# Nine and seven ring places, other stage ends, a moved low part, and the last expert behind the overflow branch, in a fused two-block kernel

## The reference, cut to what matters

```
first block:   x += pool_mixer(rms_norm(x));   x += hier_moe(rms_norm(x))        layer 0: pool, moe0
               x += mla_attention(rms_norm(x)); x += hier_moe(rms_norm(x))       layer 1: mla, moe1
               x = rms_norm(x, final_norm)
second block, for each of 2 layers (ffn00, mix0, ffn01 | ffn10, mix1, ffn11):
    x = x + 0.5 * rmsnorm(swiglu(rmsnorm(x, g0)), g1)          D_FF = 2816
    x = x + rmsnorm(mixer(rmsnorm(x, g2)), g3)                 4 attention heads, 4 mLSTM heads
    x = x + 0.5 * rmsnorm(swiglu(rmsnorm(x, g4)), g5)
hier_moe: top-1 of 4 groups, top-2 of its 8 experts; each expert (silu(h @ gate) * (h @ up)) @ down, 1024 x 512
```

## Time and profile before

| | us |
|---|---|
| time, median of 3 runs | 2138.51 |
| lowest, highest | 2137.9, 2140.11 |
| the profiled execution | 2138.28 |
| its span, first to last instruction | 2136.5 |
| PE busy | 1972.4 (92%) |
| DVE, ACT, POOL busy | 824.0, 627.5, 50.8 |

### The profile page before, as it was taken

One profiled execution on the slowest core, in us unless ns is written; L12 is line 12 of the kernel. 1 busy time (PEld: TensorE's weight loads), 2 busy tenths in 40 slices (PEclk: granted clock), 3 DMA queues, 4 the chain that ended last, 5 costly groups with the idle time before them and its releaser, 6 DMA issues.

```text
span 2136.5 us, 38361 instructions
## 1 busy us (share of the span) xinstructions
PE 1972.4 (92%) x17260; PEld 1450.9 (68%) x17260; DVE 824.0 (39%) x1263; ACT 627.5 (29%) x1016; POOL 50.8 (2%) x103
## 2 busy tenths in 40 slices
PE   6999888988989998889979999989999999999998
PEld 5544444446774444444459988879988998877996
DVE  3111111115630111111155546865545554776552
ACT  2000000004520000000054436654435444565441
POOL 0000000000000000000000000010000000010000
PEclk8999999999999999999999999999999999999999
DMA  9999999996469999999955545326545554434552
GB/s 392 414 427 428 427 428 426 428 428 245 161 237 428 426 428 428 427 427 428 426 227 201 183 162 188 119 94 221 183 172 197 190 185 170 158 103 165 185 189 79
DMA packets 56770, 599.81 MB, mean 281 GB/s; under 512 B 6544, under 2 KB 6800, under 8 KB 9488
## 3 DMA queue, kind: packets, MB, share of 16 engines
q1 hardware_dynamic: 55440, 593.79, 70.0%
q10 hardware_dynamic: 1152, 3.41, 0.6%
HBM read 596.12 MB, written 1.05 MB: 280 GB/s over the span
## 4 chain that ended last, share of the span: by engine, by line
PE 64%; DMA 21%; DVE 6%; ACT 5%; issue 3%; POOL 1%; SPq 0%; DVEq 0%; POOLq 0%; ACTq 0%
PE PS L517 14%; PE PS L519 13%; PE PS L518 13%; DMA RING<-in_w_down 11%; PE PS L660 11%; PE PS L630 6%; DMA RING<-in_w_up 4%; DMA WK<-in_w_down 3%; PE PS L605 2%; ACT SPLIT L1315 1%; DMA WK<-in_w_up 1%; ACT JK L1309 1%; PE PS L688 1%; DMA RING<-in_units 1%; DVE SPLIT L1796 1%
## 5 line engine op out<-in xcount | busy, mean ns | idle before, releaser
L1796 DVE TENSOR_TENSOR SPLIT<-RING,SPLIT 128x2048 fp32r<-128x2048 f32 (+2 forms) x178 | 400.7, 2257 | 247.1 <-ACT SPLIT L1315 246.9
L660 PE MATMUL PS<-RING,WK 128*32 128x512 f32 x816 | 373.7, 613 | 58.7 <-DMA RING<-in_w_down 38.5
L517 PE MATMUL PS<-HTH,SPLIT 128*128 128x256 f32 x1344 | 383.9, 286 | 0.0
L519 PE MATMUL PS<-HTH,SPLIT 128*128 128x256 f32 x1344 | 380.3, 283 | 0.0
L518 PE MATMUL PS<-HTL,SPLIT 128*128 128x256 f32 x1344 | 380.3, 283 | 0.0
L1315 ACT ACTIVATE SPLIT<-RING 128x2048 fp32r<-128x2048 f32 (+2 forms) x178 | 334.1, 1886 | 138.4 <-DMA RING<-in_units 129.4
L660 PEld LDWEIGHTS PS<-RING,WK 128*32 128x32 f32 x816 | 87.9, 113 | 306.8 <-issue 274.3
L517 PEld LDWEIGHTS PS<-HTH,SPLIT 128*128 128x128 f32 x1344 | 257.8, 192 | 1.9 <-issue 1.3
L518 PEld LDWEIGHTS PS<-HTL,SPLIT 128*128 128x128 f32 x1344 | 257.9, 192 | 0.5
L519 PEld LDWEIGHTS PS<-HTH,SPLIT 128*128 128x128 f32 x1344 | 257.8, 192 | 0.0
L630 PE MATMUL PS<-RING,WK 128*32 128x128 f32 x7104 | 231.0, 274 | 3.6 <-DMA RING<-in_w_up 3.2
(11 more groups left out here) (321 smaller groups left out, 2001.5 us busy)
## 6 DMA issues: line engine op xcount, KB each, us to landing
RING<-in_units SPq DMA_DIRECT2D x171, 1024.0 KB, 4.8
RING<-in_w_gate SPq DMA_DIRECT2D x56, 2048.0 KB, 25.5
RING<-in_w_up SPq DMA_DIRECT2D x55, 2048.0 KB, 26.2
RING<-in_w_down SPq DMA_DIRECT2D x53, 2048.0 KB, 29.3
WK<-in_w_down SPq DMA_DIRECT2D x9, 2048.0 KB, 31.6
WK<-in_w_up SPq DMA_DIRECT2D x9, 2048.0 KB, 26.1
WK<-in_w_gate SPq DMA_DIRECT2D x8, 2048.0 KB, 26.7
RING<-in_w_down SPq DMA_DIRECT2D x3, 1024.0 KB, 21.7
```

The source lines that it names most:

```text
L517: pe.matmul(out, ll, rh, start=start, stop=False)
L519: return pe.matmul(out, lh, rh, start=False, stop=stop)
L660: t = pe.matmul(PS[32 * i:32 * i + 32, 4 + h, :], mo.HE[:, pb, 32 * f:32 * f + 32], v[:, c, 512 * h:512 * h + 512], start=f == 0, stop=f == 3)
L1796: dv.tensor_tensor(unit_part(u, 1), loaded(u), unit_part(u, 0).bitcast(F32), ALU.subtract).then_inc(s_lo, 1)
```

## The change

It does the following.

- **The ring** has nine places in the MoE stages and seven in the others (NS = 9, HOME = 7). Two places then lie in WK, which grows from 13440 to 14112 columns. Room for it comes from the SBUF area that is set aside for dynamic DMA (`dynamic_dma_scratch_size=1024`) and from S and G, which hold two groups of four experts in turn in place of 32 experts. `places` and `gates` run for one group at steps 1, 5, 9, ...
- **The overflow branch** stands ahead of step 31 on ACT and DVE in both MoE stages, and on PE in moe0. Steps 31 and 32 (and DVE's last adds, PE's last combine) stand in both ways.
- **The entry of ffn00**: DVE's product with the final gain stands in the MoE stage, behind the adds of its own block. ACT squares X and that product before hi(u0 + 1).
- **The end of a stage**: ACT squares the PSUM row in two halves of 512, and DVE multiplies the halves with the gain row (`gains`), the two engines on different halves. The root is applied in the pass that adds to X (`add`), in two halves with semaphores of their own; ACT squares X by halves. POOL sums two partial sums. halves(1) stands ahead of hi and lo of the fifth unit; behind a mixer lo(u0 + 1) and lo(u0 + 2) are each later by one step.
- **The mixer**: lo(u0 + 14) stands behind decayed(3).
- **The last stage**: PE finishes the left half of block 1's columns first, and X leaves in four transfers.

```diff
-NS = 7
-HOME = 6
+NS = 9
+HOME = 7
+WORK = 14112
...
-        mo.S = al(2048).rearrange("p (b n) -> p b n", b=2)
-        mo.G = al(2048).rearrange("p (b n) -> p b n", b=2)
+        mo.S, mo.G = (al(512).rearrange("p (k b n) -> p k b n", k=2, b=2) for _ in range(2))
...
-                    if s == HOME and i < NS and stage == "moe1":
+                    if s >= HOME and i < NS and stage == "moe1":
...
-                sp.wait_ge(s_x, 2 * len(STAGES) - 1 + b)
-                sp.dma_start(W["out"][128 * b:128 * b + 128, :], X[:, b, :]).then_inc(s_out, 16)
+                for h in range(2):
+                    sp.wait_ge(*((s_x, 2 * len(STAGES) - 1 + b) if h else (s_xh, 2 * len(SECOND) - 1 + b)))
+                    sp.dma_start(W["out"][128 * b:128 * b + 128, 512 * h:512 * h + 512],
+                                 X[:, b, 512 * h:512 * h + 512]).then_inc(s_out, 16)
...
+            def inverse_rms_of_halves(out, halves, q, after, done):
+                po.wait_ge(*after)
+                po.tensor_scalar(out, halves[0], halves[1], q * EPS, ALU.add, ALU.add).then_inc(own.up(), 1)
+                po.wait_ge(own.sem, own.n)
+                po.tensor_tensor(out, out, MH[:, 0:1], ALU.pow).then_inc(done, 1)
...
-            for e in range(33):
-                if e == 8:
...
+            early = 31 if l == 0 else 33
+            def end():
+                for e in range(early, 33):
+                    step(e)
+                if l == 0:
+                    combine(7)
+            for e in range(early):
+                if e == 8:
+                    over = pe.value_load(FLAG[0:1, l:l + 1], min_val=0, max_val=1)
+                step(e)
+            if l:
+                combine(7)
             with pe.If(over > 0):
+                end()
                 pe_overflow(pe, l)
+            if l == 0:
+                with pe.Else():
+                    end()
...
-            for k in range(7, 11):
-                down(k, (1,), s_unit, after if k == 10 else None)
+            if after:
+                for k in range(7, 11):
+                    down(k, (1,), s_unit, after if k == 10 else None)
+            else:
+                for h in range(2):
+                    for k in range(7, 11):
+                        hi, lo = unit_pair(u0 + 22 + k)
+                        for c in range(2):
+                            f = 2 * k + c
+                            t = three(pe, PS[:, 2 + h, :], (HFH[:, f, 128:256], HFL[:, f, 128:256]),
+                                      (hi[:, c, h * 512:h * 512 + 512], lo[:, c, h * 512:h * 512 + 512]), False, f == 21)
+                        if h:
+                            t.then_inc(s_unit, 1)
+                        elif k == 10:
+                            t.then_inc(s_half, 1)
...
+                if n < 5:
+                    x_ready(n, b)
+                    square(X[:, b, :], SM[:, b:b + 1], (s_sq, 2 * n + b + 1))
+                    return
+                for h in range(2):
+                    ac.wait_ge(*((s_x, 2 * (n - 1) + b + 1) if h else (s_xh, 2 * (n - 5) + b + 1)))
+                    square(X[:, b, 512 * h:512 * h + 512], SM[:, b + 24 * h:b + 24 * h + 1],
+                           (s_sq, 10 + 4 * (n - 5) + 2 * b + h + 1), JK[:, 512 * h:512 * h + 512], 1 / 32)
...
-                j = SECOND.index(stage)
-                ac.wait_ge(*((s_unit, end_unit(stage)) if b else (s_half, j + 1)))
-                square(PS[:, 2 * b:2 * b + 2, :], SM[:, 4 + b:5 + b], (s_psq, 2 * j + b + 1),
-                       JK[:, :].rearrange("p (a n) -> p a n", a=2))
+                j, last = SECOND.index(stage), stage == SECOND[-1] and b
+                for h in range(2):
+                    if last and h == 0:
+                        ac.wait_ge(s_half, len(SECOND) + 1)
+                    elif last or h == 0:
+                        ac.wait_ge(*((s_unit, end_unit(stage)) if b else (s_half, j + 1)))
+                    else:
+                        ac.wait_ge(s_gn, 4 * j + 2 * b + 1)
+                    square(PS[:, 2 * b + h, :], SM[:, 4 + b + 22 * h:5 + b + 22 * h], (s_psq, 4 * j + 2 * b + h + 1),
+                           JK[:, 512 * h:512 * h + 512], 1 / (32 * post_place(stage)[2]))
...
                 post(before, 1)
                 hi(u0 + 3)
                 norm(n, 1)
+                halves(stage, 1)
                 hi(u0 + 4)
-                halves(stage, 1)
             def enter(stage):
...
                     ac.activation(XS[:, b, 0:512], XS[:, b, 0:512], ACT.Copy, scale=SM[:, 2 + b:3 + b]).then_inc(s_xsa, 1)
                 hi(u0)
                 squares(n, 0)
+                gained(0)
                 hi(u0 + 1)
-                gained(0)
+                scale(0)
                 squares(n, 1)
-                scale(0)
+                halves(stage, 0)
                 gained(1)
-                halves(stage, 0)
                 hi(u0 + 2)
                 scale(1)
                 hi(u0 + 3)
...
+                for e in range(31):
+                    if e == 8:
+                        ac.wait_ge(s_flag, l + 1)
+                        over = ac.value_load(FLAG[0:1, l:l + 1], min_val=0, max_val=1)
+                    step(e)
                 with ac.If(over > 0):
+                    step(31)
+                    step(32)
...
+                with ac.Else():
+                    step(31)
+                    step(32)
...
+            def gains(stage, b):
+                j, k, last = SECOND.index(stage), post_place(stage)[0], stage == SECOND[-1] and b
+                dv.wait_ge(s_row[j % 2], 16 * (j // 2 + 1))
+                if not last:
+                    dv.wait_ge(*((s_unit, end_unit(stage)) if b else (s_half, j + 1)))
+                for h in (0, 1) if last else (1, 0):
+                    if last or h == 0:
+                        dv.wait_ge(s_psq, 4 * j + 2 * b + h + 1)
+                    dv.tensor_tensor(XS[:, b, 512 * h:512 * h + 512], PS[:, 2 * b + h, :], RB[:, k, 512 * h:512 * h + 512],
+                                     ALU.mult).then_inc(s_gn, 1)
+            def add(stage, b):
                 j = SECOND.index(stage)
-                row = RB[:, post_place(stage)[0], :].rearrange("p (a n) -> p a n", a=2)
-                dv.wait_ge(s_row[j % 2], 16 * (j // 2 + 1))
+                dv.wait_ge(s_gn, 4 * j + 2 * b + 2)
                 dv.wait_ge(s_prs, 2 * j + b + 1)
-                dv.scalar_tensor_tensor(XS[:, b, :].rearrange("p (a n) -> p a n", a=2), PS[:, 2 * b:2 * b + 2, :],
-                                        SM[:, 6 + b:7 + b], row, ALU.mult, ALU.mult).then_inc(s_pt, 1)
-                dv.wait_ge(s_pt, 2 * j + b + 1)
                 dv.wait_ge(s_fin, 2)
-                dv.tensor_tensor(X[:, b, :], X[:, b, :], XS[:, b, :], ALU.add).then_inc(s_x, 1)
+                for h in range(2):
+                    x = X[:, b, 512 * h:512 * h + 512]
+                    dv.scalar_tensor_tensor(x, XS[:, b, 512 * h:512 * h + 512], SM[:, 6 + b:7 + b], x, ALU.mult,
+                                            ALU.add).then_inc(s_x if h else s_xh, 1)
             def boundary(before, stage):
                 n, u0 = STAGES.index(stage), UNIT[stage]
-                lo(u0)
-                lo(u0 + 1)
-                post(before, 0)
+                early = 2 if before[:3] == "ffn" else 1
+                for u in range(u0, u0 + early):
+                    lo(u)
+                gains(before, 0)
+                add(before, 0)
                 norm_tail(n, 0)
-                lo(u0 + 2)
+                lo(u0 + early)
                 halves(stage, 0)
-                post(before, 1)
+                gains(before, 1)
+                if early == 1:
+                    lo(u0 + 2)
+                add(before, 1)
                 lo(u0 + 3)
                 norm_tail(n, 1)
+                halves(stage, 1)
                 lo(u0 + 4)
-                halves(stage, 1)
...
-                for b in range(2):
-                    dv.wait_ge(s_x, 2 * n - 1 + b)
-                    dv.tensor_tensor(XS[:, b, :], X[:, b, :], RB[:, 2, :], ALU.mult).then_inc(s_fg, 1)
...
+            def places(l, g):
+                if g >= 2:
+                    dv.wait_ge(s_ga, 16 * l + 2 * g - 2)
+                for b in range(2):
+                    dv.tensor_tensor(mo.S[:, g % 2, b, :].rearrange("p (e s) -> p e s", e=4),
+                                     cs("iota")[:, 0:C].unsqueeze(1).to_broadcast([128, 4, C]),
+                                     mo.PO[:, b, 4 * g:4 * g + 4].unsqueeze(2).to_broadcast([128, 4, C]),
...
-                            places(l, 1)
                             longest(l)
-                            gates(l, 1)
+                        if e % 4 == 1 and e < 29:
+                            places(l, e // 4 + 1)
+                            gates(l, e // 4 + 1)
...
                 with dv.If(over > 0):
+                    step(31)
+                    step(32)
+                    add(7, 0)
```

(20 more changed lines are left out.)

89 lines of the change are left out of this document (40 added, 49 removed).

## The result

The changed kernel takes 2108.64 us (median of 4 runs, 2105.24 to 2111.07) against 2139.31 us for the kernel before, measured beside it: a ratio of 0.9856, 95% interval 0.9839 to 0.9873. (Beside the later runs the kernel before took 2139.82 to 2140.47 us.) The profiled execution took 2108.3 us with a span of 2106.4; before it was 2138.28 and 2136.5. So 30.1 us of span are gone where 35.0 were forecast, and the time lies in the range. It is 5 us above the forecast.

A forecast was written before the change was run, and what follows sets the result against it. Transfers were taken to bound the MoE stages, and PE from 1100 us on. The terms summed to 35.0 us, taking the profiled 2138.3 us to 2103.3 us, with a range of 2094 to 2114.

The forecast's parts named there:

- ring, moe1: Start of moe1: nine slabs issued ahead of the first freed place, so two fewer to move afterwards; 9.8 us gained.
- end of moe0, branch and transfers: End of moe0: 1.9 us won by the transfers, less what PE's early branch gives back; 1.2 us gained.
- entry of mla: Start of mla: ACT's branch taken ahead of step 31, so squares and PE's transposes start earlier; 1.7 us gained.
- entry of ffn00: From moe1's end to ffn00: early branch and reordered squares and product start PE's transposes sooner; 4.0 us, from 3 to 4.4.
- three starts behind ffn: Stage starts behind the three ffn stages: halves(1) moved earlier removes PE's wait of 1.13 us at each; 3.4 us gained.
- boundaries behind the mixers: Stage starts behind both mixers: waits for XS and halves(1) go, 1.2 us lost to POOL's wait; 2.5 us each, 5.0 together.
- clock behind them: Behind the second stage start, TensorE's clock returns to its upper level after shorter idle stretches; 2.0 us gained, or none.
- mixers: In the mixers, moving lo(u0+14) behind decayed(3) brings sums(2) earlier: 3.4 us in mix0, 2.5 in mix1, together 5.9.
- The lead isn't kept: Rival: something else fills the first gap of moe1, so 9.8 us are missing; 2113.1 us, chance 0.08.
- The jump at the end of the second way: Rival: this jump stalls too, 3.5 us at ffn00's entry and 1.7 at mla's; 2108.5 us, chance 0.08.
- The gaps only move: Rival: lower clock stays in the mixers and behind the stage start, POOL's wait eats the mixer boundaries; 2112.1 us, chance 0.18.
- Slower: Rival: early-branch instruction fetches queue behind weights, costing 26 us in moe0 and 26 in moe1; 2155 us, chance 0.04.

The follow-up runs named there:

- moe0_late: Changed kernel with the overflow branches of TensorE, ScalarE and VectorE back behind their last work in moe0 alone; median 2106.34 us.
- best30: Changed kernel with ScalarE's and VectorE's branches ahead of step 30 in both MoE stages, TensorE's behind its last combine in moe0; median 2104.78 us.
- ad_late: Changed kernel with ScalarE's and VectorE's branches back behind the last adds in both MoE stages, final-gain products behind the branch; median 2115.41 us.
- again: The changed kernel once more, unaltered, as yardstick and second profile; 2108.92 us.
- pe_late: Changed kernel with only TensorE's overflow branch in moe0 back behind the last combine; median 2106.25 us.
- mixlo: Changed kernel with, behind the mixers, lo(u0 + 1) between add(0) and norm_tail(0), lo(u0 + 2) ahead of halves(0), nothing between gains(1) and add(1); 2108.93 us.
- ns7: Changed kernel with the ring back at seven places in the MoE stages and six in the others (NS 7, HOME 6); median 2119.09 us.
- ns7_scratch: Changed kernel with the ring back at NS 7, HOME 6 and the dynamic DMA scratch area at its former size; median 2119.72 us.
- ns8: Changed kernel with eight ring places in the MoE stages (NS 8, HOME 7); median 2115.06 us.
- tail_back: Changed kernel with TensorE finishing block 1 of the last stage unit by unit and the stage ending like the others, output still in four transfers; 2109.32 us.

## Why the prediction held, and which steps of it didn't

The forecast was 35.0 us of gain, term by term; the table gives 30.1:

| term | forecast | table | by experiment |
|---|---|---|---|
| ring, moe1 | 9.8 | 8.9 | 10.2 to 10.5, with moe0 |
| end of moe0, branch and transfers | 1.2 | -3.35 | early branches: a loss of 1.6 (moe0_late) to 3.9 (best30) at mla's transposes |
| entry of mla | 1.7 | 1.9 | 2.5 by ad_late, 2.7 by moe0_late |
| from mla's transposes to moe1's first freed place | 0 | 2.2 | the clock for the most part; 1.4 us apart in two profiles of the same kernel |
| entry of ffn00 | 4.0 | 3.4 | 6.4 for the branch alone |
| three starts behind ffn | 3.4 | 4.0 | 6.9 for all five |
| boundaries behind the mixers | 5.0 | 4.3 | not tried as a whole |
| clock behind them | 2.0 | 1.7 | not tried |
| mixers | 5.9 | 5.0 | 4.8 to 5.1 |
| tail | 2.0 | 2.1 | 0.8 for the column order |

- **The failed step** is the 1.2 us for the end of moe0, what the transfers win there less TensorE's early branch. The last combine came 3.35 us later instead. I had charged TensorE's branch between 0 and 1.9 us, because TensorE had 2.82 us of idle time ahead of the last expert but one, and charged nothing for ScalarE's and VectorE's early branches. Four things were wrong. First, the stall is 3.67 us, more than that idle time. Second, behind it the clock was at 0.50, and the gate and up matmuls that were left took 1.5 us more. Third, the silu of expert 31 stands behind ScalarE's branch: with TensorE's branch away it came behind 4.77 us of stall, and TensorE waited 2.50 for it. Fourth, the 1.9 us of the transfers hardly arrived. In the profile after, the slabs land 1.0 to 1.2 us earlier than before between 60 and 126 us, but the up slab of expert 31 (before: 488.8 us) only 0.3 to 0.8 us earlier, in this profile and in those of again, pe_late, ad_late, moe0_late and best30. TensorE's wait for the down slab of expert 30 ends at 493.48 us in best30 and at 493.87 before:

```profile
493.48 1.93 PE L679 MATMUL PS<-RING,WK 128*32 128x256 f32 x32 [0.93 <-DMA RING<-in_w_down]
```

What took back the rest isn't shown. Besides, all ten profiles with nine places have a stall near 480 us (1.6 to 2.2 us, best30's and moe0_late's included) that the kernel before doesn't have. The range of the term should have reached to minus 3.4.
- **Luck.** The 2.2 us from mla's transposes to moe1 were in no term, and most of them went with the clock. At mla's start it was at 0.50 for 6.8 us before and not at all in the changed kernel (0.8 us), near 580 us for 10.2 us before and 3.4 after (1.1 us; TensorE's mean granted clock in the whole stretch was 0.91 before and 0.96 after). Among the profiles with nine places the stretch takes 122.8 to 125.2 us, in best30 no less than before (125.0), so nothing shows that the change brings it. Without it 27.9 us of gain would be left.
- **The entry of mla**: the working gives 1.3 us (506.9 to 505.6), I wrote 1.7, and 1.9 it is.
- **The ring** was right in mechanism and size. The 0.9 us less in the two profiles is about what two profiles of one kernel differ by (0.8).
- **The entry of ffn00**: the transposes are 4.13 us nearer, 4.0 were forecast. 0.7 us is given back: the lower clock lasts 2.6 us longer behind the transposes' start than before, the eight matmuls behind the transposes take 3.76 us for 2.74, and a wait of 0.45 us for a low part follows. I had taken "the chain behind it is the same", and at half clock it isn't.
- **Behind the mixers** I put 1.2 us down for GpSimd held by a low part. It is 1.5 us, and not at XS of block 1 but one step ahead, at lo(u0 + 3), which stands behind the same add. The Trainium skill (SBUF — State Buffer, Who interferes with whom) describes this interference; by that rule, the trace agrees (0.30 us alone, 2.14 beside the low part, 1.35 where mixlo puts one).
- **The mixers** were over-sized by 0.9 us: sums(2) waits 0.86 and 0.84 us for PE behind the low part, where I had it follow directly. Part of this is offset, since the low part itself ends earlier than I had it.
- **The rivals.** *The lead isn't kept* fell: the queues were never idle in moe1 behind the restart. *The jump at the end of the second way* costs nothing that shows: in best30 and after ScalarE's hi(0) follows its last copy without a stall. *The gaps only move* was right in its smallest part alone, the clock in the mixers. *Slower* fell: the stall of an early branch, taken with the queues full, was 4.3 to 5.1 us on ScalarE and VectorE and up to 4.0 on TensorE, and not 31; the branches behind the work cost ScalarE and VectorE 3.1 to 5.0. The Trainium skill (Runtime: NRT & Kernel Launch, Instruction fetch mechanics) speaks of such a stall without a price; these rows give one.

## What to carry to other kernels

A taken branch cost ScalarE and VectorE 3 to 5 us here wherever it stood, so put it, for each engine by itself, ahead of that engine's longest wait for another one, and not merely ahead of the last piece of work. Hold the whole stall against the wait that is to cover it, and add what the clock loses behind it. When one half of a change is to take waiting time away, look for the cover of the other half in what will be left of it. In a stage that the transfers bound, a ring place more at its start is worth one slab's transfer (4.9 us here). And look at the granted clock before comparing two profiles: one fall of it is 1.4 to 1.7 us, as much as several terms of this sum.

## What the runs showed of the hardware

- An early branch on TensorE in moe0 goes with stalls in straight code far from it. In moe1 all ten profiles with that branch have 2 to 4 stalls of 1.5 to 2.6 us that end with "issue", one of them in all ten ahead of the same matmuls, the last 11 gate and up matmuls of expert 30; the three with TensorE's branch late (pe_late, moe0_late, best30) have none, and neither has the kernel before. It isn't the depth of the ring (ns7 has two) nor the scratch area (ns7_scratch two). In moe0 it is otherwise: those three have 3 or 4 stalls of 1.2 to 2.4 us as well, where the kernel before has one of 1.2. The early branch puts a second copy of two steps into TensorE's program ahead of moe1; whether the stalls come from where the code then lies wasn't tried. With nine places they cost little: moe1 takes 439.3 to 439.5 us in the three profiles without them and 439.5 to 441.0 in the seven with them.
- TensorE's granted clock fell to its lower level (0.50) around mla's start behind waits of 8.2 and 9.0 us (before, moe0_late), and behind 6.2 and 6.4 us in best30 and pe_late, but not behind the same 6.25 us in the two profiles of the changed kernel. The wait's length alone doesn't tell it.
- The clock fell behind some stalls and not behind others. In moe1 of ns8 and ns7 it was 0.50 behind stalls of 1.96 and 2.28 us, in ns7_scratch and the changed kernel 1.00 behind 1.60 and 1.46. It isn't the length alone here either: behind 2.00 us in tail_back it stayed up.
